# Start addresses of the split weights in the first products: one pair of distances for each half unit

## What is computed

```
hn = rmsnorm(concat(meta, x), norm_in_g)
P = hn @ w_in                  # 272 tokens x 8320
Pr, Pc = P[:, :4224], P[:, 4224:]
Pr = Pr + (shift(Pr) - Pr) * mu_shift
r, k, v, g_r, wl, al = split(Pr)     # a recurrence over the tokens
Bg, Cg, hc, g_c = split(Pc)          # a causal convolution of width 3
h = h + concat(y_a, y_b) @ w_out
```

## Time and profile before

| | |
|---|---|
| median of 3 runs | 2455.44 us (2454.85 to 2455.47) |
| profiled execution, its own time | 2456.71 us |
| its span, first to last instruction | 2455.0 us |
| mean granted TensorE clock | 0.999 of full speed |
| TensorE matmuls busy | 2423.2 us, 99% |
| VectorE busy | 1754.0 us, 71% |
| ScalarE busy | 1222.9 us, 50% |
| GpSimd busy | 305.0 us, 12% |
| HBM over the span | 179 GB/s |

### The profile page before, as it was taken

The page is one execution under the profiler, slowest core; times in us unless marked ns, Lnnn a source line. Parts: engine busy times, 40 slices in busy tenths (PEclk is TensorE's granted clock), DMA queues, the critical chain, the costliest instruction groups (busy, mean ns, idle before and its releaser), DMA issues.

```text
span 2455.0 us, 42669 instructions
## 1 busy us (share of the span) xinstructions
PE 2423.2 (99%) x16586; PEld 2159.6 (88%) x16586; DVE 1754.0 (71%) x2629; ACT 1222.9 (50%) x1811; POOL 305.0 (12%) x397
## 2 busy tenths in 40 slices
PE   8999999999999999999999999999999999999998
PEld 7999999788888888888888888888888888888887
DVE  8998797896767666756766678667576757676676
ACT  6555433675554455444444556545454445444545
POOL 1212114432100000000000001101010001000011
PEclk9999999999999999999999999999999999999999
DMA  8666763386567666666666665777667767776773
GB/s 219 175 162 172 198 184 89 95 228 192 174 183 194 191 185 187 189 178 187 188 189 189 182 174 165 195 194 183 195 178 193 197 180 189 190 190 181 192 195 107
DMA packets 758365, 443.53 MB, mean 181 GB/s; under 512 B 28785, under 2 KB 721137, under 8 KB 758161
## 3 DMA queue, kind: packets, MB, share of 16 engines
q1 hardware_dynamic: 752880, 430.16, 62.9%
q0 software_dynamic: 5280, 10.56, 3.3%
HBM read 437.35 MB, written 3.31 MB: 179 GB/s over the span
## 4 chain that ended last, share of the span: by engine, by line
PE 95%; DVE 3%; issue 1%; DMA 0%; ACT 0%; SPq 0%; DVEq 0%; ACTq 0%
PE bank L295 40%; PE bank L299 20%; PE bank L275 5%; PE bank L325 5%; PE bank L277 5%; PE bank L326 5%; PE bank L329 5%; PE bank L276 5%; PE bank L1875 1%; PE bank L1894 1%; PE bank L1882 1%; PE bank L1874 1%; PE bank L1895 1%; DVE splitb L260 0%; DMA rawa<-in_w_in_dram 0%
## 5 line engine op out<-in xcount | busy, mean ns | idle before, releaser
L295 PE MATMUL bank<-xx,splitb 128*128 128x512 f32 x3328 | 1165.8, 396 | 1.5 <-DVE mix L2164 0.8
L260 DVE TENSOR_TENSOR splitb<-rawb,splitb 128x1024 fp32r<-128x1024 f32 x672 | 836.4, 1258 | 391.8 <-ACT splitb L254 379.1
L254 ACT ACTIVATE splitb<-rawb 128x1024 fp32r<-128x1024 f32 x672 | 701.6, 1056 | 500.9 <-PE bank L299 349.8
L299 PE MATMUL bank<-xx,splitb 128*128 128x256 f32 x3328 | 922.2, 277 | 0.0
L295 PEld LDWEIGHTS bank<-xx,splitb 128*128 128x128 f32 x3328 | 625.2, 188 | 130.7 <-DVE mix L2164 1.1
L299 PEld LDWEIGHTS bank<-xx,splitb 128*128 128x128 f32 x3328 | 625.4, 188 | 1.6
L295 PE MATMUL bank<-oo,splitb 128*128 128x512 f32 x1008 | 343.3, 389 | 0.0
L275 PE MATMUL bank<-xhl,splita 128*128 128x258 f32 (+2 forms) x1040 | 299.9, 288 | 10.9 <-DVE splita L260 10.5
L277 PE MATMUL bank<-xhl,splita 128*128 128x258 f32 (+2 forms) x1040 | 294.0, 283 | 0.0
L276 PE MATMUL bank<-xhl,splita 128*128 128x258 f32 (+2 forms) x1040 | 293.3, 282 | 0.0
L299 PE MATMUL bank<-oo,splitb 128*128 128x256 f32 x1008 | 278.2, 276 | 0.0
(11 more groups left out here) (294 smaller groups left out, 2260.6 us busy)
## 6 DMA issues: line engine op xcount, KB each, us to landing
rawb<-in_a_w_in_dram SPq DMA_DIRECT2D x256, 512.0 KB, 4.8
rawa<-in_w_in_dram SPq DMA_DIRECT2D x130, 512.0 KB, 5.4
rawb<-in_kv_w_dram SPq DMA_DIRECT2D x128, 512.0 KB, 4.8
rawb<-in_b_w_in_dram SPq DMA_DIRECT2D x128, 512.0 KB, 5.3
rawb<-in_a_w_out_dram SPq DMA_DIRECT2D x64, 512.0 KB, 5.2
rawb<-in_b_w_out_dram SPq DMA_DIRECT2D x64, 512.0 KB, 5.1
rawb<-in_w_out_dram SPq DMA_DIRECT2D x32, 512.0 KB, 5.1
table<-in_rel_dram POOLq DMA_DIRECT2D x32, 128.0 KB, 4.4
```

The costliest lines, as they stand in the source:

```text
L254: nc.scalar.activation(self.parts(at, h)[0], self.raw_half(at, h), ACT.Copy).then_inc(hi_ready, 1)
L260: nc.vector.tensor_tensor(lo, self.raw_half(at, h), hi.bitcast(F32), ALU.subtract).then_inc(lo_ready, 1)
L295: nc.tensor.matmul(out, hi[:, w], both(k).rearrange("p a t -> p (a t)"), start=start and k == 0, stop=False)
L299: last = nc.tensor.matmul(out[:, 0:SEQ], lo[:, w], both(k)[:, 0], start=False, stop=stop and k == 7)
```

## The change

`begins` now gets the half unit too. It takes the half units that have the same first column in their order, and gives the n-th of them the n-th pair of a list, in bytes: 33 pairs for 256 columns (`META`), 34 for 272 columns (0), and one pair for all with 258 columns (`META - 2`). It returns where the high and the low part begin. The room for this adds 24 elements to `splita`, and `lo_from` goes from 1088 to 1104; `spare2` grows by the same 24, so `inv` again begins where `area` does. The second phase's `begins` only gets the new argument.

```
-            return [kept[b][:, begin:begin + HALF] for kept, begin in zip((self.hi, self.lo), self.begins(at.u))]
+            return [kept[b][:, begin:begin + HALF] for kept, begin in zip((self.hi, self.lo), self.begins(at.u, h))]
...
-        def begins(u):
-
-            first = 0 if u == U_LORA else (FIRST if u < U_IN + 4 * CT else FIRST_CONV)[(u - U_IN) % 4]
-            return (8, 24) if first else (0, 0)
+        def first_column(u):
+            return 0 if u == U_LORA else (FIRST if u < U_IN + 4 * CT else FIRST_CONV)[(u - U_IN) % 4]
+        HALVES = [(u, h) for u in range(U_WOUT) for h in range(2)]
+        OFF_256 = [(i, j) for i in (-56, -24, 8) for j in (-56, -48, -32, -24, -16, 0, 8, 16, 24, 32, 40)]
+        OFF_272 = [(i, j) for i in (8, 40, 72) for j in (8, 16, 24, 32, 40, 56, 64, 72, 80, 88, 96)] + [(24, 24)]
+        OFFSETS = {0: OFF_272, META - 2: [(-88, 8)], META: OFF_256}
+
+        def begins(u, h):
+            column = first_column(u)
+            n = [half for half in HALVES if first_column(half[0]) == column].index((u, h))
+            hi, lo = OFFSETS[column][n % len(OFFSETS[column])]
+            return column + hi // 4 + 8, column + lo // 4
 
         st = Stream(ph, "a", 3, 0, sem("begin_in"))
-        st.place_split(8472, 2112, 48, 1088, begins)
+        st.place_split(8496, 2112, 48, 1104, begins)
...
-    spare = sbuf(p2, "spare2", [P, 3072])
+    spare = sbuf(p2, "spare2", [P, 3096])
...
-    def begins(u):
+    def begins(u, h):
```

## The result

The changed kernel takes 2461.32 us, median of 17 runs (2458.98 to 2463.82), against 2455.44 of the kernel before in as many runs: a ratio of 1.0024 with a 95% interval of 1.0017 to 1.0030, 5.9 us slower. The forecast was 3.1 us faster, the range ended at 2460.5.

What follows compares the result with a forecast made beforehand. TensorE's matmul steps were taken to bound the first products, lengthened by where loaded weights lie against streamed tokens. Terms -3.4 - 0.9 + 1.2 + 0 = -3.1 us took 2455.44 to 2452.3 us, range 2447.5 to 2460.5.

Steps and rivals of the forecast that it cites:

- D: First products, 258 columns, 1,536 matmuls moved from (-88, -24) to (-120, 8): 0 us, bounds -2.0 and +8.3.
- the rival for slower: The new 258 column pair is bad and takes the 256 column excess, +8.3 us; whole +5.2, 2460.6 us; chance 0.17.
- A: First products, 256 columns, 768 matmuls: excess falls to that of 258 columns on a 0.82 share, -3.4 us.
- B: First products, 272 columns, 816 matmuls: step falls from 123 to 121.7 ns, -0.9 us.
- C: First products, 40 new boundaries between pairs, each 0.03 us for the pace to settle: +1.2 us.
- E: ScalarE and VectorE write the parts at other addresses: costed at nothing, as neither would make TensorE wait.
- F: Buffers behind splita, including the recurrence's, move by 96 bytes: 0 us, bounds -1 and +1.
- No effect: Rival: the first products' excess belongs to width or order, not addresses; 0 us, 2455.4 us; chance 0.13.
- Cancel: Rival: one more fetch for each load that starts 8 bytes off, total within 0.2%; chance 0.11.
- the faster rival: Most first-product pairs reach the second phase's pace, -9.5 us, 2445.9, or 2447.1 with new boundaries; chance 0.24.

Runs made afterwards that it cites:

- the map: Against the kernel before, blocks of four half units with one pair each for 256 and convolution-unit 258 columns, four 272 column pairs in turn; 2456.69 us, one run.

## Why the prediction was wrong

**D failed, and with it the sum.** "Both are odd multiples of 8 before and after, so I take 0" was the step. Measured it is +5.67 us, 3.7 ns a step over 1,536 matmuls, and undoing it alone gives 5.5 us back (the 258 column sums of the change and of the kernel with the old pair). It was the rival for slower, with the right mechanism and place. That its sum, +5.2 us and 2460.6, is the trace's +5.20 and within 0.8 us of the measured time was luck: its price of 5.4 ns a step, taken from 256 columns, was too high by a half (+8.3 us for +5.67), and gains of 3.1 us that came only to some 0.5 made up for it. Its chance of 0.17 was too low for a step that carried half of all matmuls and rested on three points. The parity that A, B and D rested on is no rule: the map has pairs with the same parity at 2.773 and at 2.880 us.

**A** had the sign and not the size: -1.40 against -3.4 us. The list averages 2.836 us a half unit; no half unit comes nearer than 2.78 to the 2.75 that the text took for a good class. Its share of 0.82, by which the price falls on the steps beside a high load, isn't borne out either. In the map, 258 columns at (-88, -24) step by 123, 121 and 116 ns from the starts of L275, L276 and L277, where the good pair (-56, 8) has 115 or 116 for all. By the earlier trace rows the first of these runs beside a high load and the second beside a low one, and the third, beside the other high load, costs nothing. **B** had the wrong sign, +0.93. **C** can't be told from A and B. With one pair for each width the 256 columns won 1.17 us, or 1.56 without a wait that came with it, against 1.40 with 33 pairs, but the pairs differ as well. In the map the first half unit of a block, behind another width, differs from the settled ones by -0.011 to +0.045 us, so 0.03 was a possible price and no constant.

**E and F held.** ScalarE's L254 waited for L277 for 139.2 us in 78 times in the changed kernel, where it was 132.5 in 75; TensorE had no wait in the first products after 50 us, and the kernel moved by 32 bytes, with the same 96 bytes of room, keeps every settled length. But the cover of E was thinner than the text made it. It looked at the splits in the row units; the wait that came once TensorE was earlier than in the kernel before, if only by tenths of a microsecond (0.2 us with the old 258 column pair and the lists, 0.9 with (-56, -48) for 256 columns), is for VectorE's evacuation in a convolution unit. Had the gains come as forecast, a part of them would have gone there.

**No effect** is refuted: nothing but addresses differs between the changed kernel, the kernel with the old 258 column pair and the one before. So the Trainium skill's rule in "TensorE: Matmul & The Clock Gate", Part 2, that loading the next weights doesn't take read bandwidth from the running matmul, doesn't describe these runs: high weights moved alone by 32 bytes cost 107 ns in 24 matmuls, and moved together with the tokens nothing. That the two reads collide is my reading of it; what was shown is only that the step depends on both start addresses, and on what ran before.

**Cancel** is refuted as I put it, one more fetch for each load that starts 8 bytes off: the fastest pair of 256 columns starts so. Moving everything by 8 bytes did cost, by 1 to 4.5 ns a step, but 16 bytes, after which the weights start on a 16 byte boundary again, cost 258 columns more than 8 did.

A slip that changes nothing: the text's sum for the faster rival is 2447.1, and the lower end of its range is written 2447.5.

The prediction read the step correctly and named the lever. Its fault was to turn one good class among three into a rule, where width, address and parity all changed from class to class.

## What to carry to other kernels

Where TensorE is the bound and weights are loaded for every matmul, read the start to start step over 24 or more matmuls for each shape, not the modelled length: equal work can differ by 4 to 5% with the start addresses. Don't derive a good address from a few classes, and don't pick it from single stretches between others; use it throughout, and look again whether the engine behind still keeps up. And when a change has one part that is spread over many values and one that puts a single value on most of the work, the second carries the risk.

## What the runs showed that I had not expected

The pace has several settled states. The same instructions at the same addresses take 2.880 or 2.853 us a half unit by what ran ahead, those of (-56, -48) 2.773 or the pace of 2.880. Within a block of one pair the state is kept to some nanoseconds, over 96 matmuls for (-64, -32). What selects it wasn't found. A common move of 32 bytes leaves the lengths as they are; moves of 8 and 16 don't.

The recurrence behind the first products isn't as steady. From the last matmul of the first products to the first one of the output projection it took 75.2 us in the trace of before, 73.0 in that of the change, 72.5 in that with the old 258 column pair and 75.4 in that moved by 32 bytes, with the same instructions. Over all 14 traces it lies between 72.5 and 75.4. TensorE's idle times there add up to 7.4 us in the trace of before and to 5.4 in that of the change. Most end with "issue", and come and go in steps of some 0.27 us: ahead of one and the same matmul it is 0.73 us in these two and 1.00 in the kernel moved by 32 bytes. Two rows of the timeline of before and one of the change:

```profile
418.48 0.26 PE L1160 MATMUL bank<-kr,bkc 64*64 64x32 f32 x5 [0.28 <-issue]
...
451.36 0.25 PE L1224 MATMUL bank<-zz,inv 32*32 32x64 f32 x3 [0.62 <-issue]
```

```profile
476.32 0.25 PE L1232 MATMUL bank<-zz,inv 32*32 32x64 f32 x3 [0.59 <-issue]
```

The place of the second, 0.62 us before L1224, has none in the change. What the issue waits for there wasn't tried, and no kernel has two traces here. The difference is enough for the 2 us by which the profiled execution of the change is off, and it is why the sums above were taken over the first products alone and the verdicts from the runs.
